# Up and gate pairs of two feed-forward layers as seven products of block sums instead of eight block products

## What is computed

```python
def _swiglu(h, w_in, w_out):
    up, gate = jnp.split(h @ w_in, 2, axis=-1)
    return (jax.nn.silu(gate) * up) @ w_out
```

## Time and profile before

| | |
|---|---|
| median of 3 runs | 1863.44 us |
| lowest and highest run | 1854.42 and 1864.21 us |
| span of the profiled execution | 1855.8 us (its only recorded time) |
| PE busy | 1763.6 us, 95% of the span, 9896 matmuls |
| PEld, DVE, ACT, POOL busy | 77%, 38%, 33%, 39% |
| feed-forward of layer 0, regular pairs and down tiles | 620.8 to 1136.9 us |
| feed-forward of layer 1, the same | 1499.5 to 1838.7 us |

### The profile page before, as it was taken

The page is one execution under the profiler, slowest core; times in us unless marked ns, Lnnn a source line. Parts: engine busy times, 40 slices in busy tenths (PEclk is TensorE's granted clock), DMA queues, the critical chain, the costliest instruction groups (busy, mean ns, idle before and its releaser), DMA issues. The chain is left out here.

```text
span 1855.8 us, 24627 instructions
## 1 busy us (share of the span) xinstructions
PE 1763.6 (95%) x9896; PEld 1423.8 (77%) x9896; DVE 696.3 (38%) x1206; ACT 620.4 (33%) x893; POOL 715.3 (39%) x371
## 2 busy tenths in 40 slices
PE   5999999899899999999999999999977999999997
PEld 2888767455487888888888887777766878888886
DVE  2134354666567611101110137770178751111114
ACT  2522322555434521112211225542336452132124
POOL 1342200166545633223232336243324764345335
PEclk8999999999999999999999999999989999999999
DMA  9322232355412122212121124422200323333322
GB/s 349 78 57 57 57 125 91 102 170 174 123 46 69 51 68 76 68 57 60 53 80 57 57 81 130 130 66 57 80 1 27 110 72 107 93 90 113 91 74 74
DMA packets 212012, 163.38 MB, mean 88 GB/s; under 512 B 17742, under 2 KB 191022, under 8 KB 211926
## 3 DMA queue, kind: packets, MB, share of 16 engines
q1 hardware_dynamic: 210144, 160.92, 28.8%
q10 hardware_dynamic: 1782, 1.28, 0.3%
HBM read 160.08 MB, written 2.10 MB: 87 GB/s over the span
## 5 line engine op out<-in xcount | busy, mean ns | idle before, releaser
L2593 POOL TENSOR_TENSOR wsplit<-ring,wsplit 128x1024 fp32r<-128x1024 f32 (+1 forms) x140 | 338.6, 2431 | 521.9 <-ACT wsplit L1592 521.7
L765 PE MATMUL ps<-hhi,wsplit 128*128 128x512 f32 (+1 forms) x1920 | 473.6, 354 | 6.3 <-DVE hu L2235 6.3
L765 PEld LDWEIGHTS ps<-hhi,wsplit 128*128 128x128 f32 x1920 | 316.6, 188 | 58.6 <-DVE hu L2235 6.9
L765 PE MATMUL ps<-hlo,wsplit 128*128 128x512 f32 x976 | 295.0, 355 | 0.0
L765 PE MATMUL ps<-uhi,wsplit 128*128 128x512 f32 x1008 | 250.6, 353 | 0.0
L1592 ACT ACTIVATE wsplit<-ring 128x1024 fp32r<-128x1024 f32 (+1 forms) x140 | 139.2, 1024 | 173.5 <-PE ps L765 173.5
L2314 DVE TENSOR_TENSOR hu<-sg,ps 128x768 f32<-128x768 f32 (+1 forms) x40 | 32.8, 821 | 438.0 <-ACT sg L1661 438.0
L765 PEld LDWEIGHTS ps<-uhi,wsplit 128*128 128x128 f32 x1008 | 165.8, 188 | 26.9
L765 PEld LDWEIGHTS ps<-hlo,wsplit 128*128 128x128 f32 x976 | 161.6, 189 | 25.7
L2138 DVE SCALAR_TENSOR_TENSOR xT<-ps,modc,xT 128x512 f32<-128x512 f32 x96 | 60.6, 659 | 253.1 <-PE ps L765 231.9
L1661 ACT ACTIVATE sg<-ps 128x768 f32<-128x768 f32 (+1 forms) x40 | 28.3, 707 | 377.0 <-PE ps L765 377.0
(11 more groups left out here) (405 smaller groups left out, 2716.3 us busy)
## 6 DMA issues: line engine op xcount, KB each, us to landing
ring<-in_ffn_w_in SPq DMA_DIRECT2D x88, 512.0 KB, 3.8
ring<-in_mod_w SPq DMA_DIRECT2D x77, 512.0 KB, 4.6
ring<-in_ffn_w_out SPq DMA_DIRECT2D x32, 512.0 KB, 3.6
ring<-in_m_w_in SPq DMA_DIRECT2D x24, 512.0 KB, 3.8
ring<-in_ab_w_in SPq DMA_DIRECT2D x21, 512.0 KB, 4.0
ring<-in_ffn_w_out SPq DMA_DIRECT2D x16, 384.0 KB, 3.2
mod_rest<-in_mod_w SPq DMA_DIRECT2D x10, 512.0 KB, 15.7
ring<-in_ab_w_out SPq DMA_DIRECT2D x8, 512.0 KB, 4.5
```

Source lines behind the costliest of these rows:

```text
L765: mm = pe.matmul(dst[:, a:b], w, h[:, a:b], start=st, stop=sp_)
L2593: pool.tensor_tensor(w_part(s, 1)[:, 0:width], ring[:, (NB[f"ffn{l}"] + s) % RING, 0:width], w_part(s, 0)[:, 0:width].bitcast(F32), ALU.su ...
```

## The change

Twenty of the 22 pairs of each layer (all but the two late ones) are computed by a seven-product scheme for a 2 x 2 block product. The blocks of the weight are A11, A12 (up, first and second half of the 1024 input features) and A21, A22 (gate); those of the input are B11, B12, B21, B22 (feature half by token half). With

- S1 = A21 + A22, S2 = S1 - A11, S4 = A12 - S2, S3 = A11 - A21,
- T1 = B12 - B11, T2 = B22 - T1, T3 = B22 - B12, T4 = B21 - T2,

the seven products are A11 B11, A12 B21, S1 T1, S2 T2, S4 B22, S3 T3 and A22 T4, in this order and each in a PSUM bank of its own. Each is over 4 chunks and half the tokens: 4 x 3 matmuls of 384 tokens in layer 0 and of 256 in layer 1, so 84 per pair. Seven additions from PSUM put the up and gate tiles together.

- **DVE** makes the four weight sums S1, S2, S4 and S3 of every pair (`op_sum`, 128x512), the low parts of S1 and S3 (`op_low`), the seven combinations (`combine`, one operand in PSUM, 128x384 or 128x256), the product with silu in two halves, now with both operands in SBUF, and the low part of the hidden block.
- **POOL** makes the low parts of A11, A12, S2, S4 and A22, 128x512 each.
- **ACT** makes seven high parts (128x512), copies the first product out of PSUM, applies silu in two halves and makes the hidden block's high part. The residual scaling moves from POOL to ACT.
- **The input operands** (seven, raw, high and low) are made once per layer, during and after the LayerNorm: in layer 1 all by DVE and ACT; in layer 0 POOL makes T3 and the low parts of B22 and T3, and T4 is made in two steps.
- **Groups:** `THIRDS` becomes `GROUPS` of 4, 4, 4, 4, 2 and 4 hidden blocks (the first holds the two late ones), so 8 down tiles follow each of six groups; DVE's `z_update`s double to 48 per layer, over tiles half as long or shorter. The operands of the next pair are made while a pair runs; those of a group's first pair while the down tiles run.
- The loops of all engines over the feed-forward network are written out; some semaphores are merged.

The core of the difference:

```diff
-THIRDS = ((0, 8), (8, 8), (16, FC - 16))
+GROUPS = ((0, 4), (4, 4), (8, 4), (12, 4), (16, 2), (18, 4))
...
+        def pair_products(l, p, before):
+            for i in range(7):
+                bank = half(i)[:, 0:N2[l]]
+                if before is None:
+                    pe.wait_ge(late_gate if i in (2, 3, 6) else late_val, 2 * l + (1 if i < 4 else 2))
+                elif before[0] == "pair" and i == 0:
+                    pe.wait_ge(p_act, 3 * (PB[l] + before[1]) + 1)
+                elif before[0] == "pair":
+                    pe.wait_ge(ev, 7 * (PB[l] + before[1]) + EV[BANK_READ[i]])
+                elif i % 2 == 0:
+                    pe.wait_ge(z_ev, z_no(l, before[1], 4 + i // 2))
+                if i in LOD_RANK:
+                    pe.wait_ge(s_lod, 2 * (PB[l] + p) + LOD_RANK[i])
+                else:
+                    pe.wait_ge(s_lo, 5 * (PB[l] + p) + LO_RANK[i])
+                if p == 0 and i > 1:
+                    pe.wait_ge(*lo_wait(l, i))
+                for k in range(KH):
+                    if p == 0 and i < 2:
+                        pe.wait_ge(*lo_wait(l, i, k))
+                    w_hi, w_lo = (w_op(p, i, a)[:, k * P:(k + 1) * P] for a in range(2))
+                    mm = three(bank, ((w_hi, h_op(l, i, 0)[:, k, :]), (w_lo, h_op(l, i, 1)[:, k, :])), k == 0, k == KH - 1)
+                mm.then_inc(prod, 1)
...
+        def op_sum(l, p, o):
...
+            x, y, op = {S1: (a21, a22, ALU.add), S2: (w_raw(p, S1), a11, ALU.subtract),
+                        S4: (a12, w_raw(p, S2), ALU.subtract), S3: (a11, a21, ALU.subtract)}[o]
+            dve.tensor_tensor(w_raw(p, o), x, y, op).then_inc(s_raw, 1)
...
+            needs, reads, dst, x, y = {
+                "C11": (A12, None, up, gate, bank(A12)),
+                "U2": (S2, None, gate, gate, bank(S2)),
+                "U4": (S2, "U2", up2, gate, bank(S1)),
+                "C12": (S4, "U4", up2, up2, bank(S4)),
+                "U3": (S3, "U2", gate, gate, bank(S3)),
+                "C22": (S3, "U3", gate2, gate, bank(S1)),
+                "C21": (A22, "C22", gate, gate, bank(A22))}[what]
...
+                if kind == "pair":
+                    more = behind[0] == "pair"
+                    combine(l, i, "C11")
+                    if pair_before:
+                        pair_product(l, i - 1, 0)
+                    combine(l, i, "U2")
+                    combine(l, i, "U4")
+                    if pair_before:
+                        pair_low(l, i - 1)
+                    if more:
+                        op_sum(l, i + 1, S1)
+                        op_sum(l, i + 1, S2)
+                    combine(l, i, "C12")
+                    if more:
+                        op_sum(l, i + 1, S4)
+                    combine(l, i, "U3")
+                    combine(l, i, "C22")
+                    if more:
+                        op_sum(l, i + 1, S3)
+                        op_low(l, i + 1, S1)
+                    pair_product(l, i, 1)
+                    if more:
+                        op_low(l, i + 1, S3)
+                    combine(l, i, "C21")
```

More of the change, by code:

```diff
@@ L355, in first_mod @@
         return mod_first[:, n, :] if n < 6 else mod_rest[:, n - 6, :]
-    N_IN0, N_OUT, N_FFN, N_IN1 = 22, KD, sum(2 * nj + KD for _, nj in THIRDS), 24
+    SEQ = []
+    for g, (j0, nj) in enumerate(GROUPS):
+        SEQ += [("pair", j - N_LATE) for j in range(max(j0, N_LATE), j0 + nj)] + [("down", g)]
+    FFN_UNITS = [("late", s, 0) for s in range(2 * N_LATE)]
+    for kind, i in SEQ:
+        FFN_UNITS += [("up", i, 0), ("gate", i, 0)] if kind == "pair" else [("down", i, q) for q in range(4)]
+    N_IN0, N_OUT, N_FFN, N_IN1 = 22, KD, len(FFN_UNITS), 24
+    N_SP = 2 * N_LATE + 4 * NG
     N_FX, N_Q, MOD_PRE = 4, 2, 3
@@ L1141, in _ @@
+        def ffn(l):
+            late_tiles(l)
+            before = None
+            for kind, i in SEQ:
+                if kind == "pair":
+                    pair_products(l, i, before)
+                else:
+                    down_tiles(l, i, before[1])
+                before = (kind, i)
         pe.wait_ge(att_n, H_MLA)
@@ L2621, in ffn @@
-            full = sum(2 * nj + KD for _, nj in THIRDS[:2]) + 2 * THIRDS[2][1]
-            low(FB[l] + 5, 0, UNIT)
-            low(FB[l] + 6, 1, UNIT)
-            for k in range(KD):
-                residual_chunk(2 * l, k)
-                if k in (2, 4):
-                    low(FB[l] + 6 + k // 2, 1 + k // 2, UNIT)
-            with pool.Fori(KD // 4, full // 4) as it:
-                for s in range(4):
-                    low(it * 4 + (FB[l] + s + 1), s, UNIT)
-            w = THIRDS[2][1] * P
@@ new lines, in ffn @@
+            op_low(l, 0, A22)
+            for at, (kind, i) in enumerate(SEQ):
+                behind = SEQ[at + 1] if at + 1 < len(SEQ) else (None, 0)
+                if behind[0] == "pair":
+                    for o in (A11, A12, S2, S4, A22):
+                        op_low(l, behind[1], o)
+                elif behind[0] == "down":
+                    for q in range(4):
+                        down_low(l, behind[1], q)
+                else:
+                    for m in range(KD):
+                        if l == 0 and m in (4, 6):
+                            fx_low(m // 2 - 2)
+                        ln_sum(2 * l + 1, m)
```

841 lines of the change are left out of this document (533 added, 308 removed).

## The result

The changed kernel took 1884.91 us (median of 4 runs, 1882.62 to 1887.4), the one before 1861.99 beside it (4 runs): a ratio of 1.0142, 95% interval 1.0114 to 1.0171.

The account below looks back on a forecast made before the run. It took PE, busy 95% of the span, as the bound. Layer 0 -13.7, layer 1 +26.1 (both including PE's -60.6 saving) and clock +3 gave +15 on 1863.4: 1878 us, range 1845 to 1903.

Parts of the forecast that it names:

- PE per matmul: Feed-forward matmuls: 0.119 us for 256 tokens, 0.1735 assumed for 384; fewer matmuls save 60.6 us if PE never waits.
- DVE and POOL on the port: A two-SBUF instruction of DVE and one of POOL never run together; once DVE has had to wait, they take turns.
- A pair of layer 1: Layer 1 pairs inside groups: DVE and POOL work exceeds PE's 10.0 us, costing +33 us in the layer.
- Mid-group periods of layer 1 at 10 to 11: Sign that the forecast is wrong; it expected layer 1 pairs in mid-group 13 us apart.
- P: Period of a layer 1 pair inside a group: taken as 13.0 us, bounds 11.1 and 13.9.
- The waits before the down tiles: Layer 1: PE waits for the last hidden block, 1 us each, 2.5 for the group of two, 6 in all.
- every wait counts: Rival: P is 13.9 and each PE wait over 3 us halves the clock behind it; 1900 us, chance 0.12.
- A pair of layer 0: Layer 0 pairs: 11.6 of 14.57 us can't overlap, so only small waits, +4 us (0 to 8).
- Start of layer 0: Layer 0's first products wait for operands made in turn by DVE and POOL: +24 us (7 to 30).
- Start of layer 1: Layer 1's fifth product waits for sums, operand steps, corrections and low parts: +12 us (10 to 16).
- Clock: PE's clock falls after the last wait at each layer's start, 1.5 us each: +3 us (0 to 8).
- Hidden: ACT's list and 24 more z_updates per layer, 0.63 to 1.1 us, fit beside PE's work; no cost.

Follow-up runs that it names:

- e1: Changed kernel with POOL's low parts of A11, A12 and A22 made 16 columns wide instead of 512, except in each layer's first pair: 1864.81 us (one run).
- e10: Changed kernel with one row of DVE's list moved: S1's low part right behind the sum S4. 1861.36 us, ratio 1.0004 to the kernel before the change.
- e3: Changed kernel with DVE making low parts A11, A12, S2, S3, A22, POOL S1 and S4, and DVE's list re-ordered: 1851.98 us, ratio 0.9947 to the kernel before.
- e7: Changed kernel with e3, e6 and both layers' starts re-ordered, layer 0's T3 and low parts of B22, T3 on DVE: 1839.1 us, ratio 0.9883 to the kernel before.
- e9: Changed kernel with e3's owners of low parts but DVE's other pair rows in the old order, added low parts put between: 1894.66 us (one run).
- e6: Changed kernel with the sum of squares of layer 0's last group moved from POOL to DVE: 1880.92 us (one run).

## Why the prediction was right, and where it was not

- **PE per matmul.** Right. The assumed 0.1735 us for 384 tokens gave 14.57 us a pair, and layer 0's pairs inside a group start 14.6 apart. In layer 1 undisturbed pairs take 10.1, not 10.00.
- **DVE and POOL on the port.** Right, and borne out by e1. After DVE was held up once the engines took turns, as rows 4 and 5 had shown. The rule of the Trainium skill ("SBUF — State Buffer", "Who interferes with whom") said that they exclude each other; who gets the port next once both have work queued had to come from the rows.
- **A pair of layer 1.** The cost was right: 6 us a group forecast, 6.0, 5.9, 5.9 and 7.0 found; over the whole layer behind its first pair +33 was forecast and +35 measured (391.8 - 46.0 for the start below, less PE's own 310.4), the clock's part included. But it lies otherwise than I drew it: the periods inside a group were 10.1, 10.4 and 14.3 us, and none was 13. Over PE's own they cost 0, 0.3 and 4.2, with 1.5 in the fourth, and the 4.2 are the 2.47 us wait and the clock behind it. "Mid-group periods of layer 1 at 10 to 11" was to be a sign that the forecast is wrong, and two of three periods are there; that the sum over a group still came to 6 is in part luck. What failed is the reading of P. The forecast treats 13.0 as a length, with 11.1 as a lower bound from what can't overlap. e10 keeps every instruction and its owner and runs at 10.1: the bound of 11.1 holds for a period in which all of this must fit, but a group has slack around it, and what does not fit inside came out beside its down tiles, as 1.9 us. Of the 35 us, 18.8 were that one row of the list came late; e3's order and owners took 10.4 more. The prediction did name that row ("PE's third product (S1) waits for the last of the chain"), and didn't ask whether its place could be another. Two sums beside it do not come out either. The waits before the down tiles, "1 us each, 2.5 for the group of two", make 7.5 for six groups and not 6; measured were 1.58 us at the group of two, 0.35 at the last and none over 0.1 at the others. And the 40 that the rival "every wait counts" gives the two starts is 46 by the 30 and 16 given for them.
- **A pair of layer 0.** +4 forecast. From the first pair's end (68.4 us after the cut) the rest of layer 0 cost 9.2 us over PE's own 459.9: waits of 1.77, 3.05 and 0.88 and, after the second, 6.8 us at half clock. Mis-sized by 5, nearly all of it at the second pair, and 4.8 us of it went with e10's row.
- **Start of layer 0.** +24 forecast; the first pair ended 68.4 us after the cut at 586.1, where before's work alone gives 635.4 - 590.0 = 45.4, so +23.0. **Start of layer 1**: +12 forecast, measured the same way 46.0 - 32.8 = +13.2.
- **Clock.** +3 was too small. PE ran at half clock for 23.9 us from 621.8 and 13.7 from 1499.0, but stood idle in much of both, and found more waits behind what it did slowly. The cost is in the stretches of 3.4 us at half clock in layer 1, four behind waits of 2.5 us and one behind 3.46, about 1.5 us each, in 6.8 us at the second pair of layer 0, and in the handover. I had taken 2.64 us as harmless from one row.
- **Hidden.** This step failed, for the `z_update`s. It set 24 more updates beside tiles of 1.4 to 4.2 us and counted their duration alone. In layer 0's last group each update has a sum, a low part and POOL's sum of squares with it, and 4.2 us is less than these take in turns: +8.9 us with the clock. Nothing in the forecast looked at that group, though the number of its blocks was in the diff.
- **Sum.** Forecast +15, measured +26 in the profiled run and +23 between the medians. The surplus is the handover, 9, and the two layers, 4 each, less the 3 charged to the clock and the 4 us by which the stretch ahead was shorter.
- **Forecast of the page.** PE busy was to be 1705 and was 1729.6; a matmul at half clock is busy for longer. In e7, with few waits, it was 1713.3.

Of the rivals, none came. "Every wait counts" (1900) is nearest on the clock, but the fall costs about 1.5 us and came behind one wait of two in the groups of layer 1, and waits of 2.5 us were enough, where it asked for 3.

## What to carry to other kernels

Bounds from the sum of two engines' times on a shared port say whether a change is risky, not what it costs; the cost is how late the one row comes that the fastest engine needs next, and a queue that runs in order makes it wait for every held-up row ahead. So ask first of a loss of this kind where that row stands: moving one line (e10) gave back 23.5 us, and moving work between engines so that another needed row came late (e9) lost 10 more. And when a change gives a stage shorter pieces, count all that the other engines do for each piece, at the stage's end above all.

## What the runs showed of the hardware

- In the changed kernel PE waited 2.45 us before the third product at 1651.37 and again at 1820.47. The first wait was followed by 3.4 us at half clock, the second by none; one of 2.48 at 1833.26 was again followed by half clock. A length of wait that is safe can't be read from one row:

```profile
1651.30:1654.80 3.50, 3.43 (x20) 3.46 (x21) 2.67 (x5) 1.16 (x4) 1.09 (x1) 0.68 0.58 197
1820.40:1823.90 3.50, 3.43 (x28) 3.46 (x29) 2.67 (x5) 1.15 (x4) 1.10 (x1) 1.00 0.71 219
1833.20:1836.70 3.50, 3.44 (x17) 3.47 (x18) 2.67 (x5) 1.17 (x3) 1.08 (x1) 0.54 0.66 217
```

- Turns on the port are for whole instructions, so small ones pay for large ones: DVE's 0.68 us low part takes 1.75 beside POOL's 1.28, its 128x1536 operand takes 4.96 instead of 1.75 beside POOL's of the same size.
- POOL's instructions of 16 columns took 0.34 us in the mean (e1), where those of 512 took 1.3; a narrow instruction is far from free, but it was short enough for these turns not to matter.
- The 590 us ahead of the change, with the same 3236 matmuls in before, after and e7, took 584.5 to 590.0 us in ten traces. The stretch between the layers, which no run changes, took 317.9 to 321.2. So stretches cut at the same instructions can be compared more closely than spans, but not to the last us: where after and e6 run the same work they agree within 0.1 us in layer 0 and 1.3 in layer 1.
